# Spreading the normalisation behind the FFN over seven loads of the gather loop

## The reference, cut to what matters

```python
# first block, last part
u = expert_down[idx]; v = expert_up[idx]
act = gelu(einsum("td,thkd->thk", xb, u))
x = x + einsum("thk,thkd->td", gate * act, v)
x = rms_norm(x, norm_final_w)
# second block
x = x + gt_m * rms_norm(stick_breaking_mixer(h, w_qkv, w_o), norm_g[1])
h = modulate(rms_norm(x, norm_g[2]), sh_f, sc_f)
y = swiglu_ffn(h, ffn_w_in, ffn_w_out)
x = x + gt_f * rms_norm(y, norm_g[3])      # the change is here
```

## Time and profile before

| | |
|---|---|
| median of 3 runs | 2165.18 us (2163.8 to 2165.26) |
| the profiled execution, its own time | 2160.32 us |
| its span in the trace | 2158.5 us |
| busy: PE, DVE, ACT, POOL | 1718.6, 1325.5, 893.7, 852.4 us |
| DMA over the span | 726.10 MB, mean 336 GB/s, of which gathers 536.90 MB |

### The profile page before, as it was taken

One profiled execution on the slowest core, in us unless ns is written; L12 is line 12 of the kernel. 1 busy time (PEld: TensorE's weight loads), 2 busy tenths in 40 slices (PEclk: granted clock), 3 DMA queues, 4 the chain that ended last, 5 costly groups with the idle time before them and its releaser, 6 DMA issues.

```text
span 2158.5 us, 26088 instructions
## 1 busy us (share of the span) xinstructions
PE 1718.6 (80%) x9120; PEld 1103.6 (51%) x9120; DVE 1325.5 (61%) x2912; ACT 893.7 (41%) x2385; POOL 852.4 (39%) x679
## 2 busy tenths in 40 slices
PE   7898887755666877845968775798898869988998
PEld 6783654413334524611345422354454427868997
DVE  4777558989888766566566667655555531325442
ACT  3111344443454424445465645532222243554443
POOL 1300243457575443444344443433333410134654
PEclk9998997877888898977988978899999989999999
DMA  7276699999999999999999999999999983133443
GB/s 299 88 255 223 254 418 410 417 394 397 418 409 389 417 417 419 417 379 418 402 418 418 419 419 419 419 419 418 419 417 419 402 310 124 50 132 119 181 177 117
DMA packets 115698, 726.10 MB, mean 336 GB/s; under 512 B 13168, under 2 KB 14192, under 8 KB 44400
## 3 DMA queue, kind: packets, MB, share of 16 engines
q0 software_dynamic: 73728, 536.90, 60.7%
q1 hardware_dynamic: 41840, 187.54, 22.9%
HBM read 720.20 MB, written 2.10 MB: 335 GB/s over the span
## 4 chain that ended last, share of the span: by engine, by line
PE 44%; DMA 24%; DVE 15%; ACT 7%; issue 6%; POOL 4%; DVEq 0%; SPq 0%; POOLq 0%; ACTq 0%; PEldq 0%
PE ps L948 43%; DMA arena<-in_experts,arena_u 24%; DVE arena L2498 7%; POOL arena L2132 3%; ACT arena L1805 1%; DVE arena L2189 1%; ACT sel L1801 1%; ACT L1801 1%; DVE arena L2339 1%; DVE arena L2192 0%; POOL r_high L2159 0%; ACT L1649 0%; DVE arena L2338 0%; DVE selu L2220 0%; DVE selu L2209 0%
## 5 line engine op out<-in xcount | busy, mean ns | idle before, releaser
L948 PE MATMUL ps<-arena 128*128 128x256 f32 (+4 forms) x6088 | 1284.7, 511 | 375.6 <-ACT arena L1805 339.3
L948 PEld LDWEIGHTS ps<-arena 128*128 128x128 f32 (+2 forms) x6088 | 750.7, 173 | 864.2 <-ACT arena L1805 429.0
L2132 POOL DMA_INDIRECT arena<-in_experts,arena_u x512 | 593.9, 1160 | 819.7 <-PE ps L948 728.0
L2498 DVE CUSTOM_DVE_ANT_0 arena<-arena 128x1024 f32<-128x1024 f32 x512 | 649.5, 1274 | 385.8 <-DMA arena<-in_experts,arena_u 377.0
L1801 ACT ACTIVATE sel<-sel 128x1 f32<-128x1 f32 x512 | 102.9, 201 | 731.9 <-DVE sel L2498 717.0
L2159 POOL TENSOR_TENSOR r_low<-middle,r_low 128x1024 fp32r<-128x1024 f32 x48 | 123.5, 2578 | 240.9 <-ACT r_low L1957 240.8
L1805 ACT ACTIVATE arena<-arena,sel 128x32 f32<-128x32 f32 x512 | 164.5, 321 | 17.1 <-ACT sel L1801 0.3
L948 PE MATMUL ps<-r_low 128*128 128x256 f32 (+1 forms) x1104 | 140.8, 291 | 2.7 <-ACT r_low L2029 2.7
L948 PEld LDWEIGHTS ps<-r_low 128*128 128x128 f32 x1104 | 138.3, 192 | 5.0 <-ACT r_low L2029 3.0
L1794 ACT ACTIVATE arena<-consts,arena 128x32 f32<-128x32 f32 x512 | 120.7, 308 | 0.0
L948 PE MATMUL ps<-arena,consts 128*32 128x512 f32 (+5 forms) x672 | 90.7, 465 | 12.5 <-POOL arena L2113 4.9
(11 more groups left out here) (247 smaller groups left out, 1476.2 us busy)
## 6 DMA issues: line engine op xcount, KB each, us to landing
arena<-in_w_front SPq DMA_DIRECT2D x88, 512.0 KB, 4.9
middle<-in_w_late SPq DMA_DIRECT2D x18, 2048.0 KB, 8.0
arena<-in_w_ada SPq DMA_DIRECT2D x48, 512.0 KB, 4.9
arena<-in_w_qkv SPq DMA_DIRECT2D x48, 512.0 KB, 5.1
arena<-in_w_late SPq DMA_DIRECT2D x22, 1024.0 KB, 13.6
arena<-in_w_late SPq DMA_DIRECT2D x30, 512.0 KB
arena<-in_experts,arena_u POOLq DMA_INDIRECT x512
x<-in_x SPq DMA_DIRECT2D x4, 512.0 KB, 8.8
```

The costliest lines, as they stand in the source:

```text
L948: return nc.tensor.matmul(out_, lhsT, rhs, start=start, stop=stop_, skip_group_check=skip)
L2132: nc.gpsimd.indirect_dma_start(ring[n % RING], None, a["experts"], bass.IndirectOffsetOnAxis(ap=idxq[:, i % 4, k:k + 1], axis=0),).then_in ...
L2498: nc.vector.tensor_tensor_reduce(r[:, 0:D], r[:, 0:D], xrep[k % 4], 1.0, 0.0, ALU.mult, ALU.add, dots[:, n % 8:n % 8 + 1]).then_inc(s["dot ...
```

## The change

The stage `br` behind the FFN is cut up. ACT takes the square of tile 0 behind weight 500, that of tile 1 behind weight 501, and the root with its table loads behind weight 502 (`b2`, `b2`, `b3`). DVE does the reciprocal and tile 0's product behind dot 503, tile 0's add behind dot 504, tile 1's product behind dot 505 and its add behind dot 506. Tile 2's transposes and modulation stand at load 508 instead of 504. No instruction is added except that `br` is now written as `b2` and `b3`.

```diff
-TURN_AT = {264: 0, 267: 1, FFN_END + 7: 2}
+TURN_AT = {264: 0, 267: 1, FFN_END + 11: 2}
...
-    act.append((FFN_END + 4, "br", 1))
-    dve.append((FFN_END + 5, "br", 1))
+    for t in range(2):
+        act.append((FFN_END + 3 + t, "b2", t))
+        dve += [(FFN_END + 6 + 2 * t, "b2", t), (FFN_END + 7 + 2 * t, "b3", t)]
+    act.append((FFN_END + 5, "b3", 0))
...
+                elif stage == "b2":
+                    t = arg
+                    sc.wait_ge(s["used"], h_used("fo", FT - 1))
+                    nc.scalar.activation(h_junk[1][t], ps[:, 2 * t:2 * t + 2, :].rearrange("p b n -> p (b n)"), ACT.Square,
+                                         accum_out=stat[:, 8, t:t + 1]).then_inc(s["ysq"], 1)
+                elif stage == "b3":
+                    sc.wait_ge(s["ysq"], 8)
+                    nc.scalar.activation(stat[:, 9, 0:2], stat[:, 8, 0:2], ACT.Sqrt, bias=EPS, scale=1.0 / D).then_inc(s["ysq"], 1)
+                    nc.scalar.preload_act_table_set("gelu_and_others")
...
+                elif stage == "b2":
+                    t = arg
+                    if t == 0:
+                        ve.wait_ge(s["ysq"], 9)
+                        own.step(nc.vector.reciprocal(stat[:, 9, 0:2], stat[:, 9, 0:2]))
+                    y = ps[:, 2 * t:2 * t + 2, :].rearrange("p b n -> p (b n)")
+                    own.step(stt(h_dst[t], y, stat[:, 9, t:t + 1], gtrow[:, 1, :], ALU.mult, ALU.mult))
+                elif stage == "b3":
+                    t = arg
+                    tt(x[:, t, :], x[:, t, :], h_dst[t], ALU.add).then_inc(s["fin"], 1)
```

## The result

The changed kernel takes 2172.59 us in the median of 20 runs (2166.86 to 2179.93), the kernel before 2166.67 us in 20 runs beside them (2158.49 to 2174.67). The ratio is 1.0026, 95% interval 1.0017 to 1.0036: slower by 5.6 us, 3.7 to 7.8. Forecast were 2170.4 us and +5.2 us.

The account below looks back on a forecast made before the run. The prediction took the place to be bound by gather bytes, the loop's end by gather 511's landing. Landing +3.3 and clock +1.9 make +5.2 us on the median 2165.18, so 2170.4 us; range 2168.8 to 2172.8, 8-in-10 range 2164.8 to 2173.8.

Parts of the forecast that it names:

- The place is bound by bytes: Last gathers: landings come 2.49 us apart at 425 GB/s; DVE's block delays the dots, not the landings.
- The earlier issue of loads 510 and 511: POOL's last two gather issues: 4.6 us earlier, but the queue is full, so only 0.31 us gained.
- Landings +3.3: Last gathers: SP's value weights go out beside them, so gather 511 lands 3.3 us later; bounds 2.8 to 3.7.
- The rule used for it: Gathers beside SP's loads: from 3.7 us behind SP's issue, 4 KB rows lengthen each landing by half.
- even shares of bytes: DMA queues: rival that queues share by bytes, or the low clock lasts longer; +8 to +10 us, 6 in 100.
- The clock +1.9: PE from sums 511 on: low clock adds 0.87 us there and half of 2.06 on the rotation.
- the bound of +4.7: PE's clock: upper bound if sums 511, the rotation and a quarter of the values' 7.13 us run low.
- the product needs no wait: DVE behind dot 503: ACT's root is ready in time for tile 0's product, so DVE does not wait.
- dots 503 to 508 come at 2.49 us throughout: DVE's dots: sign expected in the profile, 2.49 us between landings, DVE never more than a piece behind.
- its cover: Tile 2's modulation on ACT: 2.90 us hidden by the wait for gather 511; otherwise weights 509 and 510 3 us late.
- The sum: Whole kernel: +3.3 us for the landing and +1.9 us for the clock make +5.2 us, 2170.4 us.

Follow-up runs that it names:

- e1: Changed kernel with all eight value weights on SP held until sums 509; ratio 0.9997 to the kernel before.
- e3: Changed kernel with all eight value weights held until sums 509 and four extra useless matmuls on PE; ratio 0.9989 to the kernel before.
- e4: Changed kernel with tile 2's transposes put back at load 504, the norm still cut up; ratio 0.9982 to the kernel before, 0.9992 when run again.
- e5: Kernel before with only tile 2's transposes moved to load 508, the norm left in one block; ratio 1.0035 to the kernel before.
- after_again: Changed kernel run and profiled a second time, unedited; ratio 1.0028 to the kernel before.
- e2: Changed kernel with four extra useless matmuls on PE, two behind tile 2's transposes, two behind sums 509; ratio 1.0003 to the kernel before.
- e7: Changed kernel with six extra useless matmuls on PE, two behind tile 2's transposes, four behind sums 509; ratio 1.0013 to the kernel before.
- e6: Changed kernel with all value weights but the first held until sums 509; one run, 22.27 us from dot 508 to tile 3's transposes (changed kernel 26.72).

## Why the prediction was right

*The place is bound by bytes.* Right. With nothing beside them the last gathers land 2.49 us apart (e1, e3, e4), and from dot 500 to dot 508 it is 20.9 us with DVE's block and 21.0 to 21.4 with its pieces. The earlier issue of loads 510 and 511 gained what was put on it: 7.46 or 7.47 from 508 to 511 against 7.78 and 7.63, so 0.16 to 0.32 us.

*Landings +3.3.* Measured +3.24, by the mechanism named. The rule used for it, landings from 3.7 us behind SP's issue on stretched by half, holds in each profile in which all eight loads go out early. After: 1745.58 + 3.7 = 1749.28; without loads dot 511 would be at 1748.85 + 7.47 = 1756.32; 7.04 x 1.5 = 10.56, so 1759.84, and it was 1759.87. By the same steps e5 gives 1758.6 and had 1758.63; after_again, e2 and e7 come out within 0.05 us too, with an unhindered dot 508 put 4.88 us behind dot 506, as in e1 and e4. The Trainium skill ("DMA: Bandwidth & Descriptors", queues, rings and completion order) has each DMA engine take turns between its queues by packets. The trace agrees: the gaps of 3.80 and 3.76 us, with such loads beside them throughout, are near the 3.74 of one 4 KB row for each 8 KB row, where even shares of bytes would make 4.98. The prediction took a row for a packet. The page of the profile fits that: it counts 73728 packets for the 512 gathers, 144 for each, of which 128 would be the rows. e6's 1.27 us for 512 KB cannot tell the two rules apart, since by either the gathers wait for those bytes once.

*The clock +1.9.* The mechanism was right, the size too small: +2.60. I let half of the rotation run at the high clock; it ran nearly all at the low one, 2.08 + 1.85 less their overlap, 3.78 against 2.06, so +1.72 where I had taken +1.03, and sums 511 with what follows to the copy +0.88, with +0.87 forecast. In the second profile even the values lost 1.07 us to it, which the bound of +4.7 had covered. I had also added the two terms as if each stood alone; e1 shows that more than half of the loss behind dot 511 goes when the landings are early.

*Off the path.* The step "the product needs no wait" failed in one profile: the FFN's last matmuls ended 1733.33, 0.4 us behind the start of dot 502, not 1.9 us ahead of it, since they took 6.34 us and not 4.70 together with sums 499, and the reciprocal waited 1.27 us. It cost nothing on the path, as DVE was level again by dot 508. Nor did dots 503 to 508 come at 2.49 us throughout: in the changed kernel they took 13.44 us where five gaps make 12.45 (see the last section). Tile 2's modulation at load 508 had its cover, but little of it: in e1 and e3, where gather 511 is on time, it sets when sums 509 can go.

*The sum.* +5.2 forecast, +5.84 in the first pair of profiles and +7.09 in the second, +5.6 (3.7 to 7.8) in the runs. The landing was met closely; the sum came out a little low because the clock's term was.

## What to carry to other kernels

A block that the chain of waits names is worth what stops being late behind it: look at the spacing of the landings first. Where they come at the rate of the queue, as here, moving the block gains next to nothing (0.16 to 0.32 us for a block of 4.92). Then ask what the engines set free will release; here it was a prefetch that had been kept clear of the last gathers only because an engine stood waiting. A wait can also have bunched work behind which TensorE's clock is high, as it was behind the three sums in one piece here, so price what follows at the lower clock where a change spreads short pieces with idle time between them.

## What I had not expected of the hardware

A single 512 KB load issued beside a queue of gathers shows in the landings some 3.6 to 3.9 us behind its issue (an estimate, worked back from the delays of the landings in e5, e6 and the changed kernel, taking half of each gather's time as the stretch) and costs 1.27 us, about what its bytes take at the gathers' rate. In e6 five gathers had been issued and had not landed when it went out, and it delayed the second and the third of them: being issued earlier, on another queue, did not keep them clear of it.

With the clock high at sums 511, it was lost in e2 by the start of the rotation, behind the 0.72 us in which PE waits for ACT's copy; ahead of those sums PE had been idle for 2.1 us. In e7, with 0.41 us there and the same 0.72 behind, it was kept.

In all kernels there is one gap between the landings of loads 500 and 508 that is about 1 us too long: at load 501 in the kernel before and in e5 (3.46 and 3.48 us), at load 506 in eight profiles with the norm cut up (3.56 or 3.57); in the first profile of the changed kernel DVE is behind there and hides where it lies. From dot 500 to dot 508 it is 20.9 us in the former and 21.0 to 21.4 in the latter where no SP load had begun to tell. Why the gap moves was not tried and stays open. The 0.1 to 0.4 us that the norm cut up may lose there lies ahead of dot 508, outside the pieces above.
